# Stick-breaking values in 512-column blocks, and the tail of each pair of heads in the next pair's first chunk

## The reference

```python
u = h @ w_in_odd[o]                       # (256, 2048) @ (2048, 8192)
q, k, v, gate = jnp.split(u, 4, axis=-1)
# per head, z = q k^T * scale, strictly causal mask:
log_beta = jax.nn.log_sigmoid(z)
log_keep = jnp.where(mask, jax.nn.log_sigmoid(-z), 0.0)
rev = jnp.cumsum(log_keep[..., ::-1], axis=-1)[..., ::-1] - log_keep
A = jnp.where(mask, jnp.exp(log_beta + rev), 0.0)
att = A @ v
x = x + (att * jax.nn.silu(gate)) @ w_out_odd[o]
```

## Time and profile before

| what | us |
|---|---|
| median of three runs | 1645.85 |
| profiled execution | 1645.64 |
| its span | 1643.8 |
| TensorE busy | 1631.0 |
| VectorE busy | 1142.1 |
| ScalarE busy | 801.4 |
| GpSimd busy | 147.7 |
| stick-breaking stage, from its first matmul to the output projection's first | 958.2 to 1342.3 |

### The profile page before, as it was taken

The page is one execution under the profiler, slowest core; times in us unless marked ns, Lnnn a source line. Parts: engine busy times, 40 slices in busy tenths (PEclk is TensorE's granted clock), DMA queues, the critical chain, the costliest instruction groups (busy, mean ns, idle before and its releaser), DMA issues.

```text
span 1643.8 us, 25504 instructions
## 1 busy us (share of the span) xinstructions
PE 1631.0 (99%) x9352; PEld 1416.6 (86%) x9352; DVE 1142.1 (69%) x1259; ACT 801.4 (49%) x955; POOL 147.7 (9%) x103
## 2 busy tenths in 40 slices
PE   9999999999999999999999999999999999999998
PEld 7888888888888888988888888888888888888886
DVE  8855597777776787767765557767667676677643
ACT  6633434465554455445433335555554554445444
POOL 0000060000003310043100000000000004400000
PEclk9999999999999999999999999999999999999999
DMA  9666755555555554457566665555565555654453
GB/s 312 198 191 193 232 177 169 177 171 165 166 166 182 187 172 150 141 178 231 184 187 195 191 183 175 176 166 182 162 191 169 176 177 179 193 162 155 156 185 136
DMA packets 266632, 297.62 MB, mean 181 GB/s; under 512 B 9040, under 2 KB 239568, under 8 KB 266448
## 3 DMA queue, kind: packets, MB, share of 16 engines
q1 hardware_dynamic: 266432, 296.78, 57.4%
q10 hardware_dynamic: 144, 0.07, 0.0%
HBM read 294.72 MB, written 2.10 MB: 181 GB/s over the span
## 4 chain that ended last, share of the span: by engine, by line
PE 97%; DVE 1%; DMA 1%; ACT 0%; issue 0%; ACTq 0%; DVEq 0%
PE ps L269 50%; PE ps L272 25%; PE ps L312 11%; PE ps L329 5%; PE ps L415 1%; PE ps L396 1%; DVE wpair L856 1%; DMA raw<-xa_wkv 0%; PE ps L541 0%; PE ps L556 0%; PE ps L455 0%; PE ps L548 0%; DMA par<-params 0%; PE ps L406 0%; PE ps L478 0%
## 5 line engine op out<-in xcount | busy, mean ns | idle before, releaser
L856 DVE TENSOR_TENSOR wpair<-raw,wpair 128x1024 fp32r<-128x1024 f32 x544 | 695.9, 1291 | 324.1 <-ACT wpair L580 321.3
L580 ACT ACTIVATE wpair<-raw 128x1024 fp32r<-128x1024 f32 x544 | 574.7, 1059 | 694.8 <-PE ps L272 535.0
L269 PE MATMUL ps<-xpair,wpair 128*128 128x512 f32 x1920 | 607.2, 398 | 1.0 <-DVE xv L924 1.0
L272 PEld LDWEIGHTS ps<-xpair,wpair 128*128 128x128 f32 x1920 | 360.7, 188 | 85.2
L269 PE MATMUL ps<-ypair,wpair 128*128 128x512 f32 x1280 | 402.8, 396 | 2.2 <-DVE wpair L856 1.6
L272 PE MATMUL ps<-xpair,wpair 128*128 128x256 f32 x1920 | 377.5, 278 | 0.0
L269 PEld LDWEIGHTS ps<-xpair,wpair 128*128 128x128 f32 x1920 | 292.9, 189 | 2.9 <-issue 2.0
L272 PEld LDWEIGHTS ps<-ypair,wpair 128*128 128x128 f32 x1280 | 240.4, 188 | 56.8
L272 PE MATMUL ps<-ypair,wpair 128*128 128x256 f32 x1280 | 251.5, 278 | 0.0
L269 PEld LDWEIGHTS ps<-ypair,wpair 128*128 128x128 f32 x1280 | 194.9, 189 | 3.2 <-issue 2.5
L312 PE MATMUL ps<-wpair,ypair 128*128 128x512 f32 x768 | 174.4, 389 | 0.0
(11 more groups left out here) (182 smaller groups left out, 938.9 us busy)
## 6 DMA issues: line engine op xcount, KB each, us to landing
raw<-xa_wkv SPq DMA_DIRECT2D x128, 512.0 KB, 4.5
raw<-w_in_odd SPq DMA_DIRECT2D x128, 512.0 KB, 3.9
raw<-w_in_even SPq DMA_DIRECT2D x96, 512.0 KB, 3.6
raw<-xa_wq SPq DMA_DIRECT2D x64, 512.0 KB, 3.5
raw<-xa_wo SPq DMA_DIRECT2D x64, 512.0 KB, 3.7
raw<-w_out_even SPq DMA_DIRECT2D x32, 512.0 KB, 3.9
raw<-w_out_odd SPq DMA_DIRECT2D x32, 512.0 KB, 4.1
xkT<-mem SPq DMA_DIRECT2D x8, 512.0 KB, 6.9
```

Of the source, the lines that this page charges most:

```text
L269: mm(ps[:, 2 * parity + j, :], still[:, k, 0, j * P:(j + 1) * P], move[:, k].rearrange("p h n -> p (h n)"), start=(k == 0), stop=False)
L272: last = mm(ps[:, 2 * parity + j, S:2 * S], still[:, k, 1, j * P:(j + 1) * P], move[:, k, 0], start=False, stop=(k == KT - 1))
L580: fn(wpair[:, KP * p:KP * (p + 1), 0, :], raw[:, p], ACT.Copy).then_inc(hi_ready, 1)
L856: v.tensor_tensor(wpair[:, kp, 1, :], raw[:, p], wpair[:, kp, 0, :].bitcast(F32), ALU.subtract).then_inc(lo_ready, 1)
```

## The change

The eight "N" chunks of the values are replaced by two times two blocks of 512 columns, each block two chunks, computed ahead of the first and of the fifth pair of heads. The values of eight heads then stay in `sb_v`. The three other chunks of a pair (queries, keys, gate) follow each other; the logits and the softplus hang in the gate's chunk. The rest of a pair (exponentials, transposes, mixing, outputs) moves into the first chunk that follows: the next pair's queries, the next block of values, or for the last pair the output projection's first chunk. There ScalarE computes the exponentials first and the gate's sigmoid right behind them, both ahead of the second piece's split. Nothing of the stage is in a loop any more. In the output projection behind it the fourth piece of the first chunk moves two places back (`later=2`), and the addition to the residual moves behind the split of the last piece. The first block of the stage waits for one evacuation less than the chunk before did.

```diff
@@ SyncE
-            with sp.Fori(0, 8, 1) as it:
-                for j in range(4):
-                    load_chunk(it * 4 + (C_SB + j), W_ino, it * CH + j * D)
+            for i in range(8):
+                if i % 4 == 0:
+                    wide(C_SB + 4 * i, W_ino, 2 * D + i * CH, blocks=2)
+                for j, base in enumerate((0, D, 3 * D)):
+                    load_chunk(sb_chunk(i, j), W_ino, base + i * CH)
@@ TensorE
-            def out_stage(c0, ready, heads=None, hooks=()):
+            def out_stage(c0, ready, heads=None, hooks=(), later=1):
                 order = [(j, p) for j in range(2) for p in range(NP)]
                 if hooks:
-                    order[3], order[4] = order[4], order[3]
-                for j, p in order:
+                    order.insert(3 + later, order.pop(3))
+                for n, (j, p) in enumerate(order):
                     piece(c0 + j, j, p, ypair, "T", ready if j == 0 else None)
                     for at, work in hooks:
-                        if j == 0 and at == p:
+                        if at == (n if later > 1 else p if j == 0 else None):
                             work()
...
+            pe.wait_ge(xpair_ready, 24)
+            for i in range(8):
+                tail = sb_tail(i - 1, 2, 3) if i else ()
+                if i % 4 == 0:
+                    c = C_SB + 4 * i
+                    for e in range(2):
+                        for half in range(2):
+                            for p in range(NP):
+                                wide_piece(c + 2 * e + half, xpair, e, half, p, c + 1 if i and e == 0 else c + 2 * e)
+                                for at, work in tail:
+                                    if e == half == 0 and at == p:
+                                        work()
+                    tail = ()
+                chunk(sb_chunk(i, 0), sb_parity(i, 0), xpair, "T", hooks=tail, evacuated=0 if i % 4 == 0 else 1)
+                chunk(sb_chunk(i, 1), sb_parity(i, 1), xpair, "T")
+                chunk(sb_chunk(i, 2), sb_parity(i, 2), xpair, "T", hooks=((1, sb_logits(i)),))
+
+            out_stage(C_OUT1, (ypair_ready, 32), hooks=sb_tail(7, 2, 3), later=2)
@@ ScalarE
+                return ((0, sb_weights(i)), (0, sb_sigmoid(i)), (turn_at, turned), (hi_at, output_hi))
+            for i in range(8):
+                tail = sb_tail(i - 1, 2, 3) if i else ()
+                if i % 4 == 0:
+                    for t in range(4):
+                        slot(C_SB + 4 * i + t, tail if t == 0 else ())
+                    tail = ()
+                slot(sb_chunk(i, 0), tail)
+                slot(sb_chunk(i, 1))
+                slot(sb_chunk(i, 2), ((1, sb_softplus(i)),))
+            out_stage(C_OUT1, steps=sb_tail(7, 2, 2), later=2)
@@ VectorE, output stage
-                    return ((END, add_product),) + (((3, lo),) if pair else ())
+                    return ((3 if later > 1 else END, add_product),) + (((3, lo),) if pair else ())
@@ VectorE, stick-breaking stage
+            def sb_values(c, e, n):
+                def work():
+                    dve.wait_ge(piece_done, (c + 1) * 4 + 8)
+                    for r in range(2):
+                        last = v.tensor_scalar(sb_v[:, r, e * 512:(e + 1) * 512], ps[:, 2 * e + r, :], rs_col[:, r:r + 1], None, ALU.mult)
+                        last.then_inc(evac_done, 1)
...
+            for i in range(8):
+                tail = ((0, sb_weights(i - 1)), (3, sb_outputs(i - 1))) if i else ()
+                if i % 4 == 0:
+                    c = C_SB + 4 * i
+                    slot(c, tail)
+                    slot(c + 1, ((END, sb_values(c, 0, i)),))
+                    slot(c + 2)
+                    slot(c + 3, ((END, sb_values(c + 2, 1, i)),))
+                    tail = ()
+                slot(sb_chunk(i, 0), ((END, sb_queries(i)),) + tail)
+                slot(sb_chunk(i, 1), ((END, sb_keys(i)),))
+                slot(sb_chunk(i, 2), ((1, sb_softplus(i)), (2, sb_cumulate(i)), (END, sb_gate(i))))
+            out_stage(C_OUT1, steps=((0, sb_weights(7)), (2, sb_outputs(7))), later=2)
```

More of the change, by code:

```diff
@@ L193, in plain, with wide @@
                         load_chunk(it * 2 + (c0 + j), w, it * (2 * CH) + j * CH)
-            def wide(c0, w, col):
-                for e in range(4):
+            def wide(c0, w, col, blocks=4):
+                for e in range(blocks):
                     for half in range(2):
@@ L601, in features_hi, with out_stage @@
                 last.then_inc(s["in_hi"], 1)
-            def out_stage(c0, heads=None, pair=True, steps=(), after=None):
+            def out_stage(c0, heads=None, pair=True, steps=(), after=None, later=1):
                 def hi(it, j):
@@ L613, in out_stage @@
                     steps = attend(heads, XA_HEADS - 1, at=0)
-                slot(c0, steps + (((3, hi(0, 0)),) if pair else ()), swapped=bool(steps))
+                slot(c0, steps + (((3, hi(0, 0)),) if pair else ()), later=later if steps else 0)
                 slot(c0 + 1, ((3, hi(0, 1)),) if pair else ())
@@ L809, in _, with output_hi @@
-                c = it * 4 + C_SB
-                slot(c)
-                slot(c + 1)
-                slot(c + 2, ((1, softplus),))
-                slot(c + 3, ((0, weights), (2, turned), (3, gate)))
-            out_stage(C_OUT1)
+                def output_hi():
+                    act.wait_ge(s["sb_y"], i + 1)
+                    fn(ypair[:, 2 * i:2 * i + 2, 0, :], tmp[:, sb_parity(i, 2)], ACT.Copy).then_inc(s["y_hi"], 1)
+                return ((0, sb_weights(i)), (0, sb_sigmoid(i)), (turn_at, turned), (hi_at, output_hi))
@@ L1266, in outputs, with sb_gate, work, sb_outputs @@
-                def outputs():
-                    t = tmp[:, 1]
-                    dve.wait_ge(s["sb_gsig"], it + 1)
+                return work
+            def sb_gate(i):
+                def work():
+                    t = tmp[:, sb_parity(i, 2)]
+                    take(sb_chunk(i, 2), sb_parity(i, 2), t)
+                    v.tensor_tensor(t, t, rs_row2, ALU.mult).then_inc(s["sb_gate"], 1)
+                return work
+            def sb_outputs(i):
+                def work():
+                    t = tmp[:, sb_parity(i, 2)]
+                    dve.wait_ge(s["sb_gsig"], i + 1)
@@ L1277, in _ @@
-                slot(c, ((END, queries),))
-                slot(c + 1, ((END, keys),))
-                slot(c + 2, ((1, softplus), (2, cumulate), (END, values)))
-                slot(c + 3, ((0, weights), (END, gate), (3, outputs)))
-            out_stage(C_OUT1)
+                    dve.wait_ge(s["y_hi"], i + 9)
+                    v.tensor_tensor(ypair[:, 2 * i:2 * i + 2, 1, :], t,
+                                    ypair[:, 2 * i:2 * i + 2, 0, :].bitcast(F32), ALU.subtract).then_inc(ypair_ready, 1)
```

135 lines of the change are left out of this document (72 added, 63 removed).

## The result

The changed kernel takes 1648.57 us (median of 20 runs, 1646.90 to 1650.09), the kernel before 1645.84 (20 runs, 1645.61 to 1646.09): a ratio of 1.0017, 95% interval 1.0011 to 1.0023. It is 2.7 us slower; forecast was 1646.2 and a range up to 1648.5. The runs of the changed kernel also lie 3.2 us apart, those of the kernel before 0.5, and they fall into groups: four at 1646.9 to 1647.1, ten at 1648.3 to 1648.9, six at 1649.6 to 1650.1. The groups go with the granted clock: its mean over a run is 0.999 or 1.000 in the four fastest runs, 0.998 or 0.999 in the middle ones, 0.997 in all of the six slowest. The profiled execution took 1649.57 us with a span of 1647.8 and belongs to the slowest group.

What follows compares the result with a forecast made beforehand. TensorE, busy 1631.0 of 1643.8 us, was taken as the bound. Terms - 2.24 - 1.2 + 0.2 + 3.6 = + 0.4 on the profiled 1645.64 gave 1646.0, forecast as 1646.2 us for the median; range 1643.8 to 1648.5.

Steps and rivals of the forecast that it cites:

- rival C: Output projection: the clock falls while TensorE stands still about 3.5 us, adding 2 us, 1648.2 us in all; chance 0.08.
- Values in 512-column blocks: Stick-breaking values: eight half chunks replace eight "N" chunks, 2.24 us less on TensorE, bounds 2.24 to 0.
- Start of the stage: Stick-breaking stage's first block waits for evacuation of banks 0 and 1, not 2 and 3: 1.2 us less.
- The tail behind the next pair's first piece: Moved weights, transposes and mixing: transposes as late as now at no cost, except 0.2 us more once after the fourth pair.
- ScalarE's order: Weights, table load and sigmoid after the first split: next piece's split perhaps 1 us late, but hidden, so no cost.
- No loops: Stick-breaking stage as straight code instead of loops: counted as zero, bounds -0.3 to +1 us.
- The swap: Output projection's first chunk, fourth piece two places back: TensorE stalls once for the relay, 3.6 us, bounds 3.0 to 4.3.
- C's price: Cost of a clock fall in the output projection's stall: half lost for as long as the gap, estimated 2 us.
- B: VectorE's lag before each pair's transposes grows: eight pairs of 0.5 us, 4 us more, 1650.2 us; chance 0.06.
- D: Half chunks run at the plain pace, or straight-line code costs what they give: +2.2 us, 1648.4 us; chance 0.08.
- the signs that I gave for being wrong: Output projection wait absent or under 2 us, waits for the masking in most pairs, or slower matmuls behind the gap.
- A: Output projection's relay makes no stall, the next chunk's piece comes in time: -3.2 us, 1642.6 us; chance 0.12.

Runs made afterwards that it cites:

- swap_alone: Kernel before with only the output projection's fourth piece moved two places back and the additions behind the last piece's split; 1651.99 us, ratio 1.0035.
- first_squares_out: Changed kernel without GpSimd's square and accumulation of the first residual block; 1646.22 us, ratio 1.0004 to the kernel before.
- additions_sooner: `weights_first` with VectorE's second cross-attention loop written out, first relay's end behind the next chunk's second split, second block's additions right after; 1641.56 us, ratio 0.9974.
- swap_by_one: Changed kernel with the output projection's fourth piece one place back, not two, and the additions ahead of the last split; 1647.46 us, ratio 1.0007.
- relay_two_later: Changed kernel with the first residual block's copy and subtraction (relay's end) behind the next chunk's third split in the output projection; 1644.72 us, ratio 0.9994.
- weights_first: `relay_two_later` with VectorE masking a pair's weights ahead of the split of the next chunk's first piece, not behind it; 1643.22 us, ratio 0.9984.
- relay_later: Changed kernel with the first residual block's copy and subtraction behind the split of the next chunk's first piece in the output projection; 1644.95 us, ratio 0.9996.

## Why the prediction was wrong

What failed is the term of the clock: the sum has it at nothing, by the step of rival C that says "the clock should hold", and it is 1.5 us at the median of the runs. The rest of the mechanism stood, the place and size of the stall too, and two small terms were off. Of the 2.4 us between forecast and median (1646.2 and 1648.57) the clock is 1.5, by the run with the extra matmuls (1647.06); the other 0.9 are mostly the transposes and a loop. By the steps of the prediction:

- *Values in 512-column blocks*, -2.24 us: right, the pace is 0.2264 us against 0.2263.
- *Start of the stage*, -1.2: right; alone it brings 1.4.
- *The tail behind the next pair's first piece*, +0.2 once: too small, it is 0.67. The transposes were not only late by the masking's start: their second half waits for the second masking. They take 0.06 us more in every pair (0.84 for 0.78), and the fourth pair's take 1.02. I had looked at the first masking only and called its 0.06 us slack; there was none. Ahead of the stall the change gained 2.7 us where the terms say 3.2: piece 12 of the output projection starts at 1356.12, and at 1359.09 before, with the same work done by then, and 0.27 us of the difference are there at 869.85 already.
- *ScalarE's order*, nothing: right, no wait of TensorE comes from it. The load of the table takes 1.28 us (1342.18 to 1343.46) and the sigmoid starts 0.02 us behind it; a drain besides does not show.
- *No loops*, 0: 0.6 us were lost in a loop that the change does not touch, within the bounds that I gave (-0.3 to +1).
- *The swap*, +3.6: measured +3.48, each hand-over within 0.05 us of the sum but the last (TensorE at E + 9.05 for 9.2), and `swap_alone` makes the same wait. My lower bound for it, 3.0 us, does not follow from its rows: 3.6 less the 0.93 that the split loses beside GpSimd (2.15 for 1.22) is 2.7, and `first_squares_out` has 2.4 from start to start.
- *Rival C*, a chance of 0.08 and nothing in the sum: this is the step that failed. I took the 4.5 us between the last matmul and the fall at the kernel's end as if they were a constant. Here it fell 2.3 us after the last matmul, and in `first_squares_out` the clock fell with a wait of 2.3 us. One observation gives no lower bound: at the ends of the thirteen kernels' traces the fall comes 2.0 to 5.1 us after the last matmul. The two extremes are `first_squares_out`, whose last matmul ends at 1639.28, and `additions_sooner`, where it ends at 1633.01 (stretches as above):

```profile
1641.00:1641.50 0.50, 0.00 (x0) 0.00 (x0) 0.50 (x2) 0.50 (x2) 0.00 (x0) 0.78 0.00 0
...
1638.00:1638.50 0.50, 0.00 (x0) 0.00 (x0) 0.00 (x0) 0.00 (x0) 0.00 (x0) 0.59 1.03 401
```

- *C's price*, an estimate of 2 us from the gap's length: the lower level lasted longer than the gap. In the profiled execution it lasts 6.8 us (to 1371.0, 5.8 of it with TensorE at work) and costs 2.76; in `swap_alone` 6.8 too; in `first_squares_out` and `swap_by_one` 3.4, and their slower runs lie some 1.5 us above their faster ones. The middle group of the changed kernel lies 1.5 us above its lowest as well, which fits a shorter stay, but no trace shows one of its runs. That C's time, 1648.2, is so close to the median is luck: 1.5 us of clock for my 2, and 0.9 of other terms.
- *The chances*: B's 0.06 and a fourth of C and D are 0.10, not 0.09; nothing hangs on it. Of the signs that I gave for being wrong two came: the matmuls behind the gap are slower, and the transposes wait for the masking in every pair.

With these the profiled execution adds up: - 0.27 at the start of the count, - 2.70, + 3.48, + 2.76, + 0.60 in the second cross-attention are + 3.87; measured is + 3.93 (1649.57 - 1645.64). Without the clock it is 1646.8, close to the lowest group. As to the other rivals: A is out (`swap_alone`), B did occur in small (0.67 us for eight pairs), not as a backlog but as a dependence on the second masking, and D is out.

## What to carry to other kernels

A stall of TensorE has two prices, its length and what follows if the clock falls in it; a single delay seen elsewhere in the trace is no licence for the second to be zero. When a piece is moved back, count what stands between it and the next use of what it releases: the relay was as long as ever, the cover had gone from three pieces to two. And the order in an engine's queue can be worth more than the work that is saved: moving two short instructions behind three splits (`relay_two_later`) and one pair ahead of one (`weights_first`) brought back 5.4 us, clock included, where the blocks and the start were to give 3.4.

## What the runs showed of the hardware

The granted clock fell to its lower level with waits of TensorE of 2.3 and 3.3 us, and in only part of the runs of one and the same kernel: 16 of 20 in the changed kernel (3.3 us), 4 of 11 in `first_squares_out` and 6 of 11 in `swap_by_one` (2.3 us each), as their groups of times show. That alone makes runs differ by 3 us. The delay from the last matmul to the fall is no constant: 2.3 us in the changed kernel's wait, 2.7 in `swap_alone`, and 2.0 to 5.1 at the kernels' ends. In the two kernels with the 2.3 us wait the fall came 0.2 and 0.45 us after TensorE had gone on. The runs whose waits were 1.0 to 1.3 us long (relay_later, relay_two_later) show no such groups. Five unneeded float32 matmuls in the 3.3 us wait kept the clock whole, at 0.68 us each and at no cost to the time. VectorE's split and GpSimd's square each took up to twice their time side by side: 2.13 for 1.22 us, and 2.02 for 1.04 us.
